# One block for the gates and the recurrence, with products of a projection placed inside the waits, in a fused NSA and RWKV layer

## What is computed

```python
# layer 1, end of the mixer
mixed = (gate_attn * y_attn + gate_conv * y_conv) @ w_o
x = x + rms_norm(mixed, g_post_mix)
h = rms_norm(x, g_pre_mlp)            # and the MLP after it
...
# layer 2: NSA attention beside an RWKV-7 recurrence of 8 heads, 64 wide
def rwkv7_step(state, inp):
    r_t, w_t, k_t, v_t, kk_t, a_t = inp
    sa = jnp.einsum('bhvk,bhk->bhv', state, -kk_t)
    state = (state * w_t[:, :, None, :] + sa[..., None] * (kk_t * a_t)[:, :, None, :]
             + v_t[..., None] * k_t[:, :, None, :])
    y = jnp.einsum('bhvk,bhk->bhv', state, r_t)
    return state, y
...
# then: group norm of y per head, + bonus, * gate; concat with the NSA output;
# x = x + concat @ w_out; out = rms_norm(x, final_g)
```

## Time and profile before

| | us |
|---|---|
| median of 3 runs | 2754.49 (2752.94 to 2754.62) |
| the profiled execution | 2754.06 |
| its span, first to last instruction | 2752.3 |
| PE busy | 2632.0 |
| DVE busy | 1433.1 |
| ACT busy | 1043.9 |
| POOL busy | 401.4 |

### The profile page before, as it was taken

The page is one execution under the profiler, slowest core; times in us unless marked ns, Lnnn a source line. Parts: engine busy times, 40 slices in busy tenths (PEclk is TensorE's granted clock), DMA queues, the critical chain, the costliest instruction groups (busy, mean ns, idle before and its releaser), DMA issues. The chain is left out here.

```text
span 2752.3 us, 43696 instructions
## 1 busy us (share of the span) xinstructions
PE 2632.0 (96%) x18134; PEld 2074.7 (75%) x18134; DVE 1433.1 (52%) x2292; ACT 1043.9 (38%) x1911; POOL 401.4 (15%) x351
## 2 busy tenths in 40 slices
PE   7999999999989999999999998989999999899988
PEld 4887777778778888888888777866776677788766
DVE  6355443435666433464333575265667646556765
ACT  2142223323345433344324544324545545344321
POOL 3311111100000000000000000021112100456544
PEclk9999999999999999999999999999999999999989
DMA  3200111134322222222222123531111243000032
...
DMA packets 45940, 238.36 MB, mean 87 GB/s; under 512 B 4272, under 2 KB 4400, under 8 KB 24240
## 3 DMA queue, kind: packets, MB, share of 16 engines
...
## 5 line engine op out<-in xcount | busy, mean ns | idle before, releaser
L355 PE MATMUL ps<-parts,parts 128*128 128x512 f32 (+2 forms) x7896 | 1815.3, 390 | 41.6 <-DVE parts L676 12.9
L355 PEld LDWEIGHTS ps<-parts,parts 128*128 128x128 f32 x7896 | 1453.0, 190 | 396.4 <-issue 35.6
L336 DVE TENSOR_TENSOR parts<-ring,parts 128x1024 fp32r<-128x1024 f32 x240 | 296.4, 1238 | 267.1 <-ACT parts L320 266.9
L320 ACT CAST parts<-ring 128x1024 fp32r<-128x1024 f32 x240 | 249.5, 1043 | 196.8 <-PE ps L355 137.2
L336 POOL TENSOR_TENSOR parts<-ring,parts 128x1024 fp32r<-128x1024 f32 x64 | 159.0, 2491 | 476.6 <-DVE parts L320 476.6
L1882 POOL TENSOR_TENSOR phase_data<-phase_data,stream 128x512 f32<-128x512 f32 x12 | 17.5, 1461 | 1260.2 <-PE ps L1414 1260.2
L714 DVE TENSOR_TENSOR_SCAN stream<-stream 128x513 f32<-128x513 f32 (+3 forms) x96 | 93.6, 975 | 194.9 <-ACT stream L623 194.6
L1118 DVE TENSOR_TENSOR parts<-phase_data,parts 128x512 fp32r<-128x512 f32 (+1 forms) x110 | 76.9, 700 | 183.8 <-ACT parts L1049 169.6
L1600 ACT ACTIVATE stream<-stream,phase_data 128x640 f32<-128x640 f32 (+7 forms) x128 | 93.5, 731 | 84.5 <-DVE phase_data L1806 84.0
L320 DVE CAST parts<-ring 128x1024 fp32r<-128x1024 f32 x64 | 57.3, 905 | 78.1 <-PE ps L355 66.5
L1178 DVE TENSOR_TENSOR phase_data<-phase_data,ps 128x512 f32<-128x512 f32 x48 | 33.0, 687 | 118.9 <-PE ps L355 118.9
...
## 6 DMA issues: line engine op xcount, KB each, us to landing
...
```

Source lines behind the costliest of these rows:

```text
L320: cast(self.hi(p), self.whole(p)).then_inc(self.k.hi_ready, 1)
L336: g.tensor_tensor(self.lo(p), self.whole(p), self.hi(p).bitcast(F32), ALU.subtract).then_inc(self.k.lo_ready, 1)
L355: last = pe.matmul(out, a, b, start=i == 0 and a is ah and b is bh, stop=i == len(pairs) - 1 and a is al)
```

## The change

Four groups of edits:

- Mixing stage: for mix and wo tiles after the first, DVE lowers the mix first, then does squares and residuals, and lowers weight pieces after them. The residuals of half 0 stand at four mix tiles and in pairs at wo tiles 0 and 1.
- Gates and chunks share one program block. The raw products of chunk 0 stand between the two halves of tile (v3, 3); mask and heads of chunk 0 no longer wait for that tile and use other buffers; waits on the tile replace the block's end.
- Chunks: `finish` is spread over levels 1 to 4, `centre` stands in level 4, ScalarE casts half 0 of the mixes (`cast_at`) and the first four weight pieces, DVE only subtracts (`first_split`), POOL lowers the four pieces from chunk 12 on. At the end of the loop the first output tile is issued in halves around `solve`, and the last `state_product` and `next_state` are left out. SP's order is new. The block sums of half 1 come one tile later.
- Final norm: the row sum is taken with the squares as the stationary operand, so that 512 sums stand as 128 by 4; root and reciprocal work on 4 columns, and `spread` turns them back into rows of 512 with four products. Half 0 is scaled two tiles at a time.

The diff, with the change of indentation left out:

```diff
+        with nc.Block() as block:
+            k.block = block
...
-    residual_at = {("wo", 1, 0): (0, "g_post_mix", (6,)), ("wo", 1, 1): (0, "g_post_mix", (7,))}
+    residual_at = {("wo", 1, 0): (0, "g_post_mix", (4, 5)), ("wo", 1, 1): (0, "g_post_mix", (6, 7))}
...
-    for t in range(6):
+    for t in range(4):
         residual_at["mix", 1, 2 * t + 2] = (0, "g_post_mix", (t,))
...
-                pieces.lower_ahead(v, n)
+                late = st in ("mix", "wo") and n > 0
+                if not late:
+                    pieces.lower_ahead(v, n)
+                if s == "ya" and m or (s, m) == ("wo", 0):
+                    low_mix(h, m - 1 if m else 7)
...
-                if here == ("mix", 1, 10):
+                if here == ("wo", 1, 0):
                     v.wait_ge(k.x_in[1], 32)
-                if s == "ya" and m or (s, m) == ("wo", 0):
-                    low_mix(h, m - 1 if m else 7)
                 if here in residual_at:
...
+                if late:
+                    pieces.lower_ahead(v, n)
...
             if (s, m) == ("v3", 3):
+                project(n, (0, 4))
                 chunk_raw(k, pe, chunk, 0)
+                project(n, (4, KT))
+            else:
+                project(n)
...
+            if (s, m) == ("v3", 3):
+                chunk_heads(k, a, chunk, 0)
             pieces.split_ahead(a, n)
...
-            chunk_heads(k, a, chunk, 0)
...
             if (s, m) == ("v3", 3):
-                tiles.may_read(v, n)
                 chunk_masked(k, v, chunk, 0)
...
+    b.mm = lambda c: mm[:, c % 2] if c else four_of(k.data(free_at[0], 2, 4 * P))
+    b.mab = lambda c: mab[:, c % 2] if c else four_of(k.data(free_at[1], 1, 4 * CHUNK))[:, 0]
...
+    first_split = {(12, 2): 4, (13, 2): 5, (14, 1): 6, (14, 2): 7, (14, 4): 0, (15, 1): 1, (15, 2): 2, (15, 4): 3}
...
+        sp.wait_ge(bo_in, 4)
+        sp.dma_start(k3[:, :, cols(0)], part("mix_keep", 0)).then_inc(mix_in[0], 16)
+        sp.wait_ge(done, 4)
+        x_again(0)
+        sp.wait_ge(bo_in, 8)
+        sp.dma_start(k3[:, :, cols(1)], part("mix_keep", 1)).then_inc(mix_in[1], 16)
+        sp.wait_ge(y_mm, C)
+        sp.dma_start(gate[1], part("gate_keep", 1)).then_inc(gate_in[1], 16)
+        x_again(1)
+        load_weights(k, sp, START["wout", 0] + 4)
+        x_again(2)
         load_weights(k, sp, START["end"])
...
-            pe.matmul(k.bank(7), k.const("ones"), oacc[h], start=True, stop=False)
+            for b in range(4):
+                pe.matmul(k.bank(7)[:, b:b + 1], oacc[h][:, b * P:(b + 1) * P], one, start=b == 0, stop=False,
+                          skip_group_check=True)
...
+        def spread(h):
+            pe.wait_ge(bonus_read, 8)
+            pe.wait_ge(ln_done, 8)
+            pe.wait_ge(rstd_done, rstd_0 + h + 1)
+            for b in range(4):
+                last = pe.matmul(k.bank(spread_bank[h])[:, b * P:(b + 1) * P],
+                                 rstd[h][:, b:b + 1].to_broadcast((P, P)), ident, start=True, stop=True)
+            last.then_inc(spread_mm, 1)
...
+                if c == 0:
+                    pe.wait_ge(k.in3.emptied["v"], 2 * len(IN3_TILES))
                 turn(c)
+            else:
+                project(0, (0, 4))
             if c >= 1:
                 solve(c - 1)
...
             if c == C:
+                project(0, (4, KT))
                 y_part(c - 1)
-                state_product(c - 1)
...
-            pe.wait_ge(y_read, C)
-            pe.wait_ge(s_ready, C)
-            pe.wait_ge(done, 4)
-            for n in range(16):
+        for n in range(1, 16):
             project(n)
-                if n < 4:
-                    mean(4 + n)
+            if n < 5:
+                mean(3 + n)
...
+        cast_at = {(11, 5): 4, (12, 5): 5, (13, 2): 6, (13, 5): 7, (14, 2): 0, (14, 4): 1, (14, 5): 2, (15, 2): 3}
+        a.wait_ge(k.in3.filled, 2 * len(IN3_TILES))
         exps(1)
...
+                    if l == 1 and 11 <= c < 15:
+                        pieces.split_ahead(a, 0, most=c - 10)
+                    if (c, l) in cast_at:
+                        split_hi(0, cast_at[c, l])
...
-            a.activation(root, k.bank(7), ACT.Sqrt, bias=k.eps, scale=1.0 / D).then_inc(root_done, 1)
+            a.activation(root[h], k.bank(7, 4), ACT.Sqrt, bias=k.eps, scale=1.0 / D).then_inc(root_done, 1)
...
+        def inverse_out(h):
             v.wait_ge(root_done, h + 1)
+            v.reciprocal(rstd[h], root[h]).then_inc(rstd_done, 1)
...
-                        if l == 3 and 8 <= c < 12:
-                            centre(c - 8)
                     if l == 3 and c + 1 < C:
                         masked(c + 1)
-                        if l == 2 and 10 <= c < 14:
-                            finish(c - 10)
+                    if l <= 4 and 10 <= c < 14:
+                        finish(c - 10, (l,))
+                    if l == 4 and 8 <= c < 12:
+                        centre(c - 8)
                     if l == 4 and 9 <= c < 13:
                         take_bonus(c - 9)
-                        if l == 4 and 10 <= c < 14:
-                            split_first(c - 10)
...
+                    if (c, l) in first_split:
+                        split_lo(0, first_split[c, l])
-                    if c == 15:
-                        pieces.split_ahead(v, 0)
-                else:
-                    next_state(c - 1)
...
+            if c >= 12:
+                pieces.lower(g, c - 11)
```

1395 lines of the change are left out of this document (707 added, 688 removed).

## The result

The changed kernel takes 2718.99 us (median of 4 runs, 2717.13 to 2719.52) where the kernel before takes 2754.55 (4 runs, 2752.94 to 2756.3): a ratio of 0.987, 95% interval 0.9852 to 0.9887. The profiled execution took 2718.51 us with a span of 2716.7, 35.6 us under the span before. The forecast was 2716.0, with a range of 2707 to 2729.

The account below looks back on a forecast made before the run. The prediction took TensorE, busy 2632.0 of 2752.3 us, to bound the kernel. Gains of 11.1 + 7.4 + 1.9 + 14.2 + 3.1 = 37.7 us, taken from 2754.1, gave 2716 us, range 2707 to 2729.

Parts of the forecast that it names:

- Part 1: Mixing stage of half 1: lowering the mix before the weight piece shortens DVE's turns; gain 11.1 us (8 to 12.5).
- the unit of the sum: TensorE's time per product, 0.24 us from 60 products in 14.48 us; a tile of 24 is 5.7 us.
- Part 2: Gates into chunks: half the last gate tile fills the wait for POOL, chunk 0 starts earlier; gain 7.4 us (6 to 8.5).
- Part 3: Work inside the chunks: centring, finishing steps and casts moved to other places or engines; gain 1.9 us (-1 to 4).
- Part 4: After chunk 15: first output tile in halves around solve, weights split before; gain 14.2 us (13 to 15).
- The bound beside it: After chunk 15: uncovered, DVE's combine and ScalarE's copies would cost under the 3.9 us from solve's end to the tile.
- Part 5: The end: reciprocal on four columns instead of 512, with a spreading step added; gain 3.1 us (2 to 3.8).
- The sign "under 3 us": At the end: the time from last product to first scaling should be under 3 us.
- The first: Rival, in chunks 11 to 14: shared DVE and POOL reads cost 2.4 us each, 9.6 in all, giving 2726; chance 0.11.
- the second: Rival, output stage of half 1: paired residuals delay the row sum by up to 5.7 us, giving 2722; chance 0.06.
- the third: Rival, after chunk 15: split mixes or weights not ready, the 7.3 us wait stays elsewhere, giving 2724; chance 0.07.
- the fourth: Rival, output tiles: TensorE's clock stays at 1.2 GHz, 5.7 us more per tile, up to 2807; chance 0.02.

Follow-up runs that it names:

- the run with four edits: Changed kernel with half 0's old row sum, ScalarE's first three mix casts in level 3, POOL's last four bonus inputs delayed, finishing steps respread: 2720.69 us.
- that with three edits: Changed kernel with three mix casts in level 3, finishing steps and two mix splits moved, POOL pausing between its last four bonus inputs: 2718.03 us.

## Why the forecast held, step by step

**Part 1: right in the mechanism, short by the clock.** The turn of 6.5 us is 6.44, the last group comes 11.4 us earlier (forecast 11.1, "some 11 us earlier"), the turns of DVE are three of 6.43 us and three of 4.79 (forecast 6.5 and 4.8), the last wait is 1.38 us (forecast: at most 2), the others 0.6 (under 1), and no wait stands before the row sum. The four residuals beside the output tiles cost nothing, as the run of the old stage confirms from the other side. The step that fell short is the unit of the sum: I priced idle time alone, while the 4.42 us wait also lowered the clock for some 4 us behind it. That was in the rows that I had: 75 products in 19.63 us are 0.262 us each, where 60 took 14.48, 0.241 each. I read the second for the unit and the first only for its wait. It is 2.0 us.

**A loss that no part has: 1.1 us near 1525.** Before the row sum there PE waits 3.53 us in both kernels. The clock falls behind it in both traces, but not alike: before it is at 0.50 from 1540.3 to 1543.9, behind the sum, which takes 1.13 us; after it is at 0.50 from 1524.1, while PE still waits, to 1531.2, and the sum takes 2.08 us. Windows inside the two stretches, before and after:

```profile
1540.50:1543.50 3.00, 3.00 (x9) 2.32 (x8) 2.78 (x1) 1.71 (x3) 0.00 (x0) 0.50 0.00 0
```

```profile
1524.50:1531.00 6.50, 5.29 (x11) 3.50 (x11) 3.55 (x3) 4.44 (x6) 0.00 (x0) 0.50 0.00 0
```

From this row sum to the next it is 41.05 us before and 42.13 after. Of the thirteen traces of the changed kernel and the experiments, three do not fall here at all (39.5 us, waits of 3.44 to 3.53), six fall as the kernel before did (41.1 us, waits of 3.41 to 3.58), and four fall like the changed kernel (42.0 to 42.4 us, waits of 3.46 to 3.55). Eleven of the thirteen run the same program up to this point, and all three kinds are among them, so it is chance of the execution. It took back half of what the clock gave in part 1.

**Part 2: right, 7.8 for 7.4.** Raw products to transposes: 6.36 us where I had 5.7. Two sizes were off and cancel. DVE's step that I had at 0.21 us took 0.73 beside a product of POOL, 0.5 us late. And the warm start, for which I took 0.2 of a possible 1, brought 1.2: transposes to transposes of chunk 0 take 13.42 us where they took 14.66, with a granted clock of 0.67 over the first seven. That size is not certain: in two of the thirteen traces the clock falls in chunk 0 all the same, and it takes 14.74 and 14.88 us. One block with a mask and heads that do not wait for the tile was worth 4.4 us by the run with the whole tile.

**Part 3: half of it, 0.9 for 1.9.** Plain chunks still take 15.16 us. Chunk 8 gave 0.32 (forecast 0.3), chunk 13 0.54 (0.45), chunk 15 0.84 (0.9). A quarter of a microsecond of the miss is arithmetic: the terms that I took, 0.3, 0.45, 0.3 less 0.3, and 0.9, add up to 1.65 and not to 1.9. I also named 16.4 us as the length of a chunk with extra work; chunks 9 to 12 took 17.2 to 17.9 already. Two terms were wrong. Chunk 11 became 0.38 us longer. I had the cast of a mix there at 0.3, which is right, but set the same gain against it for DVE's casts that left, and nothing came of it: ScalarE, not DVE, was last there (the run with the casts in level 3 gives 0.52 back). And chunk 14, which I took for a plain one of 15.16 us, takes 15.62. In the run with four edits it takes 15.16 once step 3 no longer stands behind the masks of chunk 13, and in that with three edits, which moves the step too, 15.31; the eleven traces with step 3 in its place have 15.35 to 15.87. I read that as late masks being passed on to the next chunk's first levels; it isn't isolated from the other edits of those runs.

The rule of the Trainium skill that spoke against the change (page "SBUF — State Buffer", section "Who interferes with whom": the later of a DVE instruction with two SBUF inputs and a GpSimd instruction that reads SBUF blocks until the first is done) is borne out by three pairs of rows here: 1.50 or 0.42 us for the state update, 2.92 or 1.07 for a finishing step, 2.74 or 0.69 for a split. What the rows add is its price for PE. The blocked row of 2.92 us cost PE 0.37 us of waiting, the one of 1.50 us 1.1 us. My rival had priced each clash at its full length, 2.4 us, and four of them; with the four casts they cost 0.15 to 0.4 us in all in chunks 11 to 14, since in most levels DVE waits for PE anyway.

**Part 4: right, 13.9 for 14.2.** From the state part's end at 2599.70 to the next tile at 2607.45 it is 7.75 us where I had 7.5, at clock 1.00. (The bound beside it was misread: from solve's end at 2628.79 to the tile at 2633.69 passed 4.9 us, not 3.9; no term rests on it.) The runs divide it: the weights split ahead bring the most (5.3 us come back without, though DVE's sum is then not behind the casts as it was before), the halves 1.1. The step that failed is its last sentence. "The other fifteen tiles and the twelve sums take the same 95 us" is off by 1.4: the row sum of half 0 lies among them, and I said of its new form that it "lies beside tiles". That is true of root, reciprocal and scaling. Its products are on PE, which has no idle time there: 1.70 + 0.81 us instead of 1.31, 1.2 us. The slack of the mixes of half 1, "about 1 us", is in truth nil: in five of the traces, that with four edits among them, PE waits 0.24 to 0.47 us for the last mix inside tile 8. That is what the prediction named as a sign of being wrong, a wait for DVE inside the output tiles. It is absent from both traces of the changed kernel itself.

**Part 5: 2.4 for 3.1.** The reciprocal is 0.18 us (0.2). DVE waits 2.10 us before it instead of 2.60, so sum and root shrink by 0.5, not 0.8. The spreading step with its hops is 1.31 us up to the scaling, not 0.9: its four products take 1.13 us, and I had priced them by the transposes, 0.66. Counted from the last tile, the scaling comes 2708.72 - 2704.24 = 4.5 us later; from the end of the sum, 2706.9, it is 1.8. The sign "under 3 us" holds only in the second count, and the prediction does not say which it means.

**The rivals.** None of them took place. The first fell by the pieces split late, the second by the old mixing stage, the third since no wait is left at 2599, the fourth since the clock is 1.00 from 2599 to 2704. But the fourth is nearer than its 0.02 says, as a fall and not as a lasting one: with 3.92 us of waiting in that place the clock fell for one half tile, and in chunk 0 it fell in two traces behind waits of at most 1.4 us.

By parts: 2.3 more in the mixing stage, 1.4 less on the way, 0.4 more at the boundary, 1.0 less in the chunks, 0.3, 1.4 and 0.7 less behind them: 2.1 us under the forecast sum, and the median lies 0.5 over the profiled execution. The mechanism of the parts held, but that the sum came so near is partly luck: the clock gave 2.0 us in part 1 and 1.0 in part 2 that I had not counted and took 1.1 near 1525, and these set off the row sum of half 0 and the two chunks.
